# Stick-breaking attention in a two-layer fp32 block: hi and lo halves stacked into one matmul operand, and a pair's two heads in step

## The reference

```python
qkv = (u @ sb_w_qkv[o]).reshape(B, S, 3, SB_HEADS, HEAD_DIM)    # u = rmsnorm(h, mix_pre_g[1])
# for each head; strict = (key position < query position)
z = q @ k.T * HEAD_DIM ** -0.5
log_beta = log_sigmoid(z)
log_1m = where(strict, log_sigmoid(-z), 0.0)
acc = cumsum(log_1m, axis=keys, reverse=True) - log_1m
w = where(strict, exp(log_beta + acc), 0.0)
o = w @ v
# all heads
mixed = o @ sb_w_out[0]
```

## Time and profile before

| | us |
|---|---|
| median of 3 runs | 1375.86 (1373.96 to 1376.29) |
| profiled execution, its own time | 1374.53 |
| profiled execution, span from first to last instruction | 1372.8 |
| TensorE busy | 1321.9 (96%) |
| VectorE busy | 730.3 (53%) |
| ScalarE busy | 543.8 (40%) |
| GpSimd busy | 275.8 (20%) |

### The profile page before, as it was taken

One profiled execution on the slowest core, in us unless ns is written; L12 is line 12 of the kernel. 1 busy time (PEld: TensorE's weight loads), 2 busy tenths in 40 slices (PEclk: granted clock), 3 DMA queues, 4 the chain that ended last, 5 costly groups with the idle time before them and its releaser, 6 DMA issues.

```text
span 1372.8 us, 17850 instructions
## 1 busy us (share of the span) xinstructions
PE 1321.9 (96%) x6663; PEld 1115.1 (81%) x6663; DVE 730.3 (53%) x980; ACT 543.8 (40%) x869; POOL 275.8 (20%) x213
## 2 busy tenths in 40 slices
PE   6877999999999999999998999999999999999997
PEld 5666888889888888888887888888898888888885
DVE  4777654527644454322387676765485544453223
ACT  5456565546322322222355444343553222322112
POOL 1433100026211111000252222222441111110002
PEclk9989999999999999999999999999999999999999
DMA  5311223122333333233221211120324333333221
GB/s 166 113 37 50 77 70 85 47 77 78 107 92 104 94 92 101 87 100 97 76 77 31 58 51 46 51 72 16 92 78 122 92 92 104 94 107 92 92 92 62
DMA packets 190499, 112.29 MB, mean 82 GB/s; under 512 B 13696, under 2 KB 184773, under 8 KB 190446
## 3 DMA queue, kind: packets, MB, share of 16 engines
q1 hardware_dynamic: 188636, 106.81, 26.7%
q0 software_dynamic: 640, 2.10, 0.6%
q10 hardware_dynamic: 1170, 2.66, 0.5%
HBM read 109.43 MB, written 4.74 MB: 83 GB/s over the span
## 4 chain that ended last, share of the span: by engine, by line
PE 86%; DVE 7%; ACT 3%; POOL 2%; issue 1%; DMA 0%; POOLq 0%; ACTq 0%; SPq 0%; DVEq 0%
PE banks L388 27%; PE banks L390 27%; PE banks L389 27%; PE banks L1626 3%; DVE w_lo L383 1%; PE banks L1409 1%; DVE u_lo L668 1%; DVE tf L658 1%; PE banks L437 1%; DVE logits L1371 0%; POOL rope_tmp L1118 0%; POOL residual L729 0%; DVE probsT_lo L1421 0%; ACT w_hi L376 0%; DVE diag L455 0%
## 5 line engine op out<-in xcount | busy, mean ns | idle before, releaser
L383 DVE TENSOR_TENSOR w_lo<-w_raw,w_hi 128x1024 fp32r<-128x1024 f32 (+2 forms) x200 | 291.5, 1460 | 274.9 <-ACT w_hi L376 274.7
L388 PE MATMUL banks<-u_hi,w_hi 128*128 128x512 f32 (+1 forms) x1112 | 425.4, 383 | 9.3 <-DVE w_lo L383 4.3
L390 PE MATMUL banks<-u_hi,w_lo 128*128 128x512 f32 (+1 forms) x1112 | 419.2, 377 | 0.0
L389 PE MATMUL banks<-u_lo,w_hi 128*128 128x512 f32 (+1 forms) x1112 | 418.9, 377 | 0.0
L376 ACT ACTIVATE w_hi<-w_raw 128x1024 fp32r<-128x1024 f32 (+2 forms) x200 | 206.0, 1031 | 245.1 <-PE banks L390 245.0
L388 PEld LDWEIGHTS banks<-u_hi,w_hi 128*128 128x128 f32 x1112 | 210.1, 189 | 49.6 <-issue 8.2
L390 PEld LDWEIGHTS banks<-u_hi,w_lo 128*128 128x128 f32 x1112 | 210.2, 189 | 38.6
L389 PEld LDWEIGHTS banks<-u_lo,w_hi 128*128 128x128 f32 x1112 | 210.4, 189 | 37.9 <-issue 1.0
L861 POOL TENSOR_TENSOR up<-up,gate 128x512 f32<-128x512 f32 x44 | 71.8, 1632 | 375.5 <-DVE up L887 358.4
L842 ACT ACTIVATE gate<-gate 128x512 f32<-128x512 f32 x44 | 27.8, 633 | 202.3 <-DVE gate L883 202.3
L1646 POOL TENSOR_TENSOR stick_lo<-stick,stick_hi 128x1280 fp32r<-128x1280 f32 x16 | 56.7, 3546 | 183.4 <-DVE stick_hi L1642 183.4
(11 more groups left out here) (248 smaller groups left out, 2054.6 us busy)
## 6 DMA issues: line engine op xcount, KB each, us to landing
w_raw<-in_ffn_w_gate_up_dram SPq DMA_DIRECT2D x88, 512.0 KB, 3.8
w_raw<-in_ffn_w_down_dram SPq DMA_DIRECT2D x30, 512.0 KB, 3.6
w_raw<-in_sb_w_qkv_dram SPq DMA_DIRECT2D x24, 512.0 KB, 3.8
w_raw<-in_ab_w_in_dram SPq DMA_DIRECT2D x17, 512.0 KB, 3.9
w_raw<-in_ffn_w_down_dram SPq DMA_DIRECT2D x16, 448.0 KB, 3.4
w_raw<-in_ab_w_out_dram SPq DMA_DIRECT2D x8, 512.0 KB, 3.6
w_raw<-in_sb_w_out_dram SPq DMA_DIRECT2D x8, 512.0 KB, 3.6
bias_by_distance<-bias_rows ACTq DMA_DIRECT2D x1, 2560.0 KB
```

The lines of the kernel that those rows point to most:

```text
L383: dve.tensor_tensor(wl[:, c.slot, 0:w], raw[:, c.slot, 0:w], wh[:, c.slot, 0:w].bitcast(F32), ALU.subtract).then_inc(w_lo, 1)
L388: nc.tensor.matmul(o, lh, rh, start=start, stop=False, skip_group_check=True)
L389: nc.tensor.matmul(o, lh, rl, start=False, stop=False, skip_group_check=True)
L390: return nc.tensor.matmul(o, ll, rh, start=False, stop=stop, skip_group_check=True)
```

## The change

**The passes.** The key tile sb_k now holds one tile for each head e: k_hi on the head's own 64 rows and k_lo on the other head's 64. The query tile sb_q_hi holds the head's q_hi on both halves of the rows. One matmul over 128 rows so gives hi by hi plus hi by lo. sb_q_lo is zero on the other half and gives lo by hi. z is two matmuls for each block instead of three. The values' transposed tile sb_v has v_hi in the head's own 64 columns and v_lo in the other 64, and is multiplied with stick_hi and with stick_lo: two matmuls instead of three, and lo by lo comes along. The output's two parts now stand on different rows and are added afterwards.

**What is added elsewhere.** ScalarE writes q_hi in four copies of 64 rows instead of two, and k_hi in two copies of 64 rows instead of one of 128. VectorE writes k_lo in two subtractions of 64 rows instead of one of 128. Instead of one so_hi and one so_lo for each pair, each head has two ScalarE copies of 64 rows (`sb_o_act`, into so_hi and sq_tile), a VectorE subtraction that frees the bank (`sb_o_read`, into sq_sum) and a VectorE addition (`sb_o_dve`, into so_lo).

**The heads in step.** softplus, nsp_hi and nsp_lo get a part for each head, the tile stick is gone (the weights' exp writes over softplus), and q and k no longer have a second buffer. The orders are rewritten: z of both heads stand together at the end of a turn, c of both heads behind each other, and pv of pair p-1 moves into turn p. stick_lo of the very last head is on VectorE instead of GpSimd. The loop covers turns 2 to 5.

```diff
-            for j in (0, 1, 3, 2):
-                w, at = T - P * j, COL_AT[j]
-                k = slice(j * P, (j + 1) * P)
-                mm3(Z[:, at:at + w], sq[2][:, par, k], sq[3][:, par, k],
-                    sq[0][:, par, e, P * j:T], sq[1][:, par, e, P * j:T], start=(j != 3), stop=False)
+        def z_products(e):
+            for j in (0, 1, 3, 2):
+                w, at = T - P * j, COL_AT[j]
+                for n, x in enumerate((qh, ql)):
+                    nc.tensor.matmul(ZB[e][:, at:at + w], ks[:, e, j * P:(j + 1) * P], x[:, e, P * j:T],
+                                     start=(j != 3 and n == 0), stop=False, skip_group_check=True)
...
+        def z_pair_pe(pe, p, par):
+            pe.wait_ge(qj_lo, p * 2 + 2)
+            pe.wait_ge(w_exp, p * 2)
+            for e in range(2):
+                z_products(e)
+                z_mask(e)
...
+        def sb_q_act(act, p, par):
...
+            for e in range(2):
+                for half_rows in range(2):
+                    ins = act.activation(qh[head_rows(half_rows), e, :], sb_tile(p, 0)[head_rows(e), :], ACT.Copy)
...
+        def sb_k_act(act, p, par):
...
+            for e in range(2):
+                ins = act.activation(ks[head_rows(e), e, :], sb_tile(p, 1)[head_rows(e), :], ACT.Copy)
...
-            values(bank(O_BANK), sv, par, e, swh[:, e, :], swl[:, e, :], 0).then_inc(sv_done, 1)
+            for j in range(TT):
+                w, at = T - P * j, COL_AT[j]
+                for n, x in enumerate((swh, swl)):
+                    mm = nc.tensor.matmul(bank(b)[:, P * j:T], sv[:, par, e, j, :], x[:, e, at:at + w],
+                                          start=(j == 0 and n == 0), stop=(j == TT - 1 and n == 1),
+                                          skip_group_check=True)
+            mm.then_inc(sv_done, 1)
...
+        def sb_o_act(act, p, e, b):
+            act.wait_ge(sv_done, p * 2 + e + 1)
+            act.activation(so_at(soh, p, e), bank(b)[head_rows(e), :], ACT.Copy)
...
+            act.activation(sqt[head_rows(e), :], bank(b)[head_rows(1 - e), :], ACT.Copy).then_inc(so_hi_s, 1)
...
+        def sb_o_dve(dve, p, e):
+            dve.wait_ge(so_read, p * 2 + e + 1)
+            nc.vector.tensor_tensor(so_at(sol, p, e), acc[head_rows(e), :], sqt[head_rows(e), :], ALU.add)\
+                .then_inc(so_lo_s, 1)
...
+        def sb_pair_pe(pe, p, par, first=False, q_next=True, last=False):
             q = 1 - par
-            if first:
-                pe.wait_ge(qj_read, 5)
...
+            if not first:
+                sb_pv_pe(pe, p - 1, q, 0, O_BANK, sb_read(p, 3))
             if last:
-                pe.wait_ge(qj_read, 4 * SB_PAIRS)
-                out_part(pe, CH_OUT1, 0, out1_at, 0, 6)
+                pe.wait_ge(so_lo_s, 2 * p - 2)
+                out_part(pe, CH_OUT1, 0, out1_at, 3, 5)
+            elif not first:
+                sb_project(pe, p + 1, 1)
+            if not first:
+                sb_pv_pe(pe, p - 1, q, 1, O_BANK, None)
+            if last:
+                out_part(pe, CH_OUT1, 0, out1_at, 5, 6)
+                pe.wait_ge(so_lo_s, 2 * p)
+                out_part(pe, CH_OUT1, 1, out1_at, 0, 7)
+            else:
+                sb_project(pe, p + 1, 2)
             c_pe(pe, p, 0)
+            c_pe(pe, p, 1)
             if last:
                 pe.wait_ge(w_exp, 2 * SB_PAIRS - 1)
-                out_part(pe, CH_OUT1, 1, out1_at, 0, 6)
+                out_part(pe, CH_OUT1, 2, out1_at, 0, 5)
+                for e in range(2):
+                    sb_pv_pe(pe, p, par, e, LAST_O_BANKS[e], sb_read(p, 3))
+                return
+            sb_vt_pe(pe, p + 1, q)
+            if q_next:
+                sb_project(pe, p + 2, 0)
+            else:
+                pe.wait_ge(so_lo_s, 6)
+                out_part(pe, CH_OUT1, 0, out1_at, 0, 3)
+            z_pair_pe(pe, p + 1, q)
...
-            sb_pv_pe(pe, SB_PAIRS - 1, 1, 1)
-            pe.wait_ge(so_lo_s, SB_PAIRS - 1)
-            for n in range(3):
-                out_part(pe, CH_OUT1, n, out1_at, *((6, 7) if n < 2 else (4, 5)))
-            out_pe(pe, CH_OUT1, 2, 2, N_POST_A1, out1_at, (so_lo_s, SB_PAIRS), (7, 7, 5))
+            out_part(pe, CH_OUT1, 0, out1_at, 6, 7)
+            out_part(pe, CH_OUT1, 2, out1_at, 5, 7)
+            out_pe(pe, CH_OUT1, 2, 2, N_POST_A1, out1_at, (so_lo_s, 2 * SB_PAIRS), (7, 7, 7))
```

More of the change, by code:

```diff
@@ new lines, in sb_project, with sb_vt_pe @@
+        def sb_project(pe, p, j, inside=None, inside_at=None):
+            if not (early(p) and j < 2):
+                pe.wait_ge(qj_read, (sb_read(p - 1, 2), sb_read(p, 0), 5 if early(p)
+                                     else sb_read(p, 1))[j])
+            c = sb_chunk(p, j)
+            pe.wait_ge(w_lo, c.n + 1)
+            project(pe, bank(sb_bank(p, j)), c, KD, P, 0, P, uh, ul, inside=inside, inside_at=inside_at)\
+                .then_inc(w_used, 1)
+        def sb_vt_pe(pe, p, par):
+            pe.wait_ge(qj_read, sb_read(p, 2))
+            if not early(p):
+                pe.wait_ge(so_read, 2 * p - 2)
+            elif p == 1:
+                pe.wait_ge(qj_read, sb_read(0, 3))
+            for t in range(TT):
+                mm = nc.tensor.transpose(bank(O_BANK)[:, t * P:(t + 1) * P], sb_tile(p, 2)[:, t * P:(t + 1) * P],
+                                         ident[:, :])
+            mm.then_inc(qj_mm, 1)
@@ L1728, in sb_pair_dve @@
-        def sb_pair_dve(dve, p, par, first=False, last=False):
-            q = 1 - par
-            if not last and not first:
-                sb_scale(dve, p + 1, q, 0)
-                sb_item_dve(dve, p + 1, q, 0)
-                sb_split_dve(dve, p + 1, 0)
-            z_dve_clamp(dve, p, 1)
+                out_part(pe, CH_OUT1, 2, out1_at, 0, 5)
+                for e in range(2):
+                    sb_pv_pe(pe, p, par, e, LAST_O_BANKS[e], sb_read(p, 3))
+                return
+            sb_vt_pe(pe, p + 1, q)
@@ L1735, in sb_pair_dve @@
             z_dve(dve, p, 1)
             ns_dve_hi(dve, p, 1)
[L1737 removed]
+            if not (first or last):
+                sb_k_dve(dve, p + 1, q)
+            if not first:
+                sb_o_read(dve, p - 1, 1, O_BANK)
             ns_dve_lo(dve, p, 1)
[L1739 to L1741 removed]
+            if not (first or last):
+                sb_q_dve(dve, p + 1, q)
             if not first:
[L1743 removed]
@@ L1758, in sb_pair_dve @@
-            w_dve(dve, p, 1, first)
+                sb_o_dve(dve, p - 1, 1)
+            if not last:
+                split_lo(dve, sb_chunk(p + 2, 0))
+                sb_scale(dve, p + 1, 2)
+                split_lo(dve, sb_chunk(p + 2, 1))
+                split_lo(dve, sb_chunk(p + 2, 2))
+            w_dve(dve, p, 0)
+            w_dve(dve, p, 1)
+            if last:
+                stick_lo(dve, nc.vector.tensor_tensor, p, 1)
+            else:
+                if q_next:
+                    sb_scale(dve, p + 2, 0)
+                sb_v_dve(dve, p + 1, q)
@@ L1760, in sb_turns, with sb_pair_pool @@
+        def sb_pair_pool(pool, p, par, first=False, q_next=True, last=False):
+            stick_lo(pool, nc.gpsimd.tensor_tensor, p, 0)
+            if not last:
+                stick_lo(pool, nc.gpsimd.tensor_tensor, p, 1)
         def sb_turns(eng, pair):
             pair(eng, 0, 0, first=True)
-            with eng.Fori(0, (SB_PAIRS - 2) // 2) as i:
-                pair(eng, i * 2 + 1, 1)
+            pair(eng, 1, 1)
+            with eng.Fori(0, (SB_PAIRS - 4) // 2) as i:
                 pair(eng, i * 2 + 2, 0)
+                pair(eng, i * 2 + 3, 1)
+            pair(eng, SB_PAIRS - 2, 0, q_next=False)
```

441 lines of the change are left out of this document (204 added, 237 removed).

## The result

The changed kernel takes 1388.49 us, median of five runs (1383.65 to 1390.35); the kernel before, 1376.22 (1373.96 to 1376.65). The ratio is 1.0087, 95% interval 1.0076 to 1.0097: 12 us slower. The forecast was 1384.4 us, range 1374 to 1392. The profiled execution after took 1390.35 us, its span is 1388.6 us; before it was 1374.53 and 1372.8.

The account below looks back on a forecast made before the run. TensorE was taken to bound the kernel, with nothing idle (30.8 us summed against 30.62 a pair). 20.8 us saved and some 29 spent on idleness and low clock: 1375.86 + 8.5 = 1384.4 us, range 1374 to 1392.

Parts of the forecast that it names:

- The saved passes: In z and pv, each dropped pass saves a third of the matmuls' time: 20.8 us of TensorE time over 16 heads.
- The turn: A middle turn costs 29.75 us instead of 30.62: 28.2 of TensorE work plus idle time.
- The two waits: In each turn TensorE idles 0.46 us for the scale of k and 1.10 for the scale of v.
- c of head 1 finds its lo ready just in time: In each turn TensorE's c of head 1 starts without waiting for VectorE's lo.
- The start: TensorE idles 6.0 us before c of pair 0's head 1, loses 1.9 to the clock; pair 1's z ends at 752.1.
- The last turn: TensorE idles 8.45 us for pair 6's so_lo and loses 1.9 to the clock; chunk 3 comes at 69.4.
- The clock: At the start and in the last turn, long idleness brings 4 us at 1.2 GHz, costing 1.9 us each.
- The sum: Over the stage, output chunk 3 starts at 970.25 instead of 961.70, so the change costs 8.55 us.
- Turns without waits: Rival: early output and q copies let a turn cost 28.2 us, the ends stay; 1375.1 us in all, chance 0.14.
- Cheap pieces: Rival: 64-row copies cost half a full one, so turns run at 28.2 us; 1369 in all, chance 0.07.
- Dearer pieces: Rival: moving rows to the other half costs 0.15 us a piece, a turn 31.2; 1396 in all, chance 0.12.
- The passes save less: Rival: weight loads stand closer, so half of the 20.8 us is saved; 1386 us in all, chance 0.05.

Follow-up runs that it names:

- e4: The kernel before with two matmul passes instead of three in z and in the product with v, nothing else changed: 1371.3 us, ratio to before 0.9965.
- e6: The changed kernel without two of ScalarE's 64-row q_hi copies a turn, from pair 2 on: 1380.9 us, ratio to the kernel before 1.0035.
- e2: The changed kernel with ScalarE's and VectorE's work reordered inside the turns of pairs 1 to 6: 1380.2 us, ratio to the kernel before 1.0027.
- e1: The changed kernel with the product of the output's second weight chunk moved behind both c's in the last turn: 1380.7 us, ratio to the kernel before 1.0040.
- e3: The changed kernel with head 1's exp, ln and sums ahead of pair 1's splits at the start: 1380.5 us, ratio to the kernel before 1.0034.
- e5: The changed kernel with the reorderings of e1, e2 and e3 together: 1363.4 us, ratio to the kernel before 0.9913.
- e10: e5 with three products of the output's second weight chunk between the last turn's two c's: 1362.1 us, ratio to the kernel before 0.9894.
- e8: e5 without two of ScalarE's 64-row q_hi copies a turn, from pair 2 on: 1363.7 us, ratio to the kernel before 0.9902.
- e9: e5 with a third pass put back in z and in the product with v: 1380.7 us, ratio to the kernel before 1.0031.
- e7: The changed kernel with a third pass put back in z and in the product with v: 1400.9 us, ratio to the kernel before 1.0185.

## Why the prediction was right

- **The saved passes.** TensorE's work in a turn is 28.2 us, as worked out: 30.12 less the 1.93 above. That the matmuls lose their full third is seen in e4. The 30.62 of the earlier trace rows is the shorter of two alternating distances, their mean is 30.69; the forecast builds on steps and not on it, so nothing in it moves.
- **The turn, forecast 29.75, measured 30.12.** The two waits are where they were put, 0.34 for the scale of k (0.46 forecast), 0.97 for the scale of v (1.10), and the loop through ScalarE's copies is what makes them (e6, e2). The step that was mis-sized: a wait costs more than its idle time, 0.16 and 0.19 us more here, and "c of head 1 finds its lo ready just in time" cost 0.27. Over five turns 1.9 us.
- **The start.** z of head 0 at 720.4: it was 721.98 with the stage 1.5 later, so right. Idle before c of head 1: 6.0 forecast, 5.2 measured, c of head 1 at 738.4, measured 740.69 - 1.5 = 739.2. The idle time came out smaller because c of head 0 began 1.6 us late, at 732.63 - 1.5 = 731.1 instead of 729.5: z of pair 0 ran in part at 1.2 GHz behind the 2.31 us wait ahead of it, which the forecast put at full clock. In e1, where it did run at full clock, c of head 1 came 0.8 us earlier behind the first scale. So z of pair 1 ended 1.6 us later than 752.1: 0.8 from that late start and 0.8 because 1.2 GHz lasted through c and beyond the transposes, some 6 us and not 4: c took 5.18 instead of 4.7, the transposes 0.7 instead of 0.38.
- **The last turn.** 8.45 us idle forecast, 8.21 measured; moving that wait (e1) took 6.5 us off, though the half clock stayed.
- **The clock.** The earlier trace rows gave the right level, and in the last turn the length: 3.95 us (947.45 to 951.4). Three more stretches at half clock were not forecast: in z of pair 0, at chunk 3 behind the 1.98 us wait for w_lo (window 974 to 978.5 above), and from 1009 us on. With the last two, the part behind chunk 3 is 3 us longer than in e1, e2, e3, e5 and e10 (410.8 to 411.1), and so it is in e8 and e9 (414.2 and 413.8); e6 and e7 have only the one at chunk 3 (412.4 and 412.3). They come and go: the five runs of the changed kernel spread over 6.7 us, and the fastest, 1383.65 us, is within 1 us of the forecast.
- **The sum.** 8.55 us in the stage forecast, 11.4 measured: 1.9 from the turns, 1.6 from the start, which leaves -0.6 for the last two turns. The median is 12.3 above before's; what of this are the stretches that come and go differs from run to run. That the median stayed inside the range owes something to its width: it lies 4.1 us above the forecast, half of the cost forecast.
- **The rivals.** "Turns without waits" describes e2, not the change. Cheap pieces fall: ScalarE's pairs of 64-row copies took 1.26 to 1.27 us after as before. Dearer pieces fall too: copies that move rows to the other half take no longer, x4 in 2.54 to 2.56 us. "The passes save less" falls in the matmuls' time.
- **The page's rule on casts.** By the Trainium skill, "SBUF — State Buffer", Who interferes with whom, the cast of head 1 delays GpSimd's first piece. The trace of after agrees: GpSimd's two pieces take 6.35 to 6.37 us, of which the first has 3.46 instead of 2.95, and in the last turn a cast is itself held:

```profile
961.20 1.78 DVE L1689 CAST stick_hi<-softplus 128x1280 fp32r<-128x1280 f32 x1 [1.93 <-ACT softplus L1683]
963.02 1.49 DVE L1693 TENSOR_TENSOR stick_lo<-softplus,stick_hi 128x1280 fp32r<-128x1280 f32 x1
```

It takes 1.78 instead of 0.83 us while GpSimd works from 959.35 to 962.30.

What stays open: why the three short stretches are at half clock in some runs and not in others. It wasn't tried.
